# Half of the tokens' cross attention and expert queries placed among the first tile's expert picks, and norms on turned sums

## The reference

```python
def first_block(x, mem, ...):
    x = x + conv_mixers(rms_norm(x, norm_mix_g), ...)
    mem_n = rms_norm(mem, norm_mem_g)                  # 256 memory rows
    x = x + memory_cross_attention(rms_norm(x, norm_xa_g), mem_n, w_q, w_kv, w_xo)   # 4 heads of 256
    x = x + peer_ffn(rms_norm(x, norm_peer_g), w_pq, subkeys, u, v)
    return rms_norm(x, final_norm_g)

def peer_ffn(h, w_pq, subkeys, u, v):
    q = einsum('bsd,dq->bsq', h, w_pq).reshape(b, s, 8, 2, 128)
    sub_scores = einsum('bshpc,pnc->bshpn', q, subkeys)
    top_s, top_i = top_k(sub_scores, 16)               # then the best 16 of the 16 x 16 sums
    fin_s, fin_pos = top_k(cand_s, 16)                 # 8 heads x 16 = 128 experts a token
    gates = softmax(fin_s)
    act = gelu(einsum('chkd,cd->chk', u[experts], h)) * gates
    return einsum('chk,chkd->cd', act, v[experts])
```

## Time and profile before

| what | value |
| --- | --- |
| median of 3 runs | 3723.98 us (3719.53 to 3728.15) |
| the profiled execution | 3720.78 us |
| its span in the trace | 3719.0 us |
| PE busy | 3313.2 us, 89% |
| DVE busy | 2575.6 us, 69% |
| ACT busy | 1516.6 us, 41% |
| granted TensorE clock, mean | 0.962 |

### The profile page before, as it was taken

The page is one execution under the profiler, slowest core; times in us unless marked ns, Lnnn a source line. Parts: engine busy times, 40 slices in busy tenths (PEclk is TensorE's granted clock), DMA queues, the critical chain, the costliest instruction groups (busy, mean ns, idle before and its releaser), DMA issues.

```text
span 3719.0 us, 48652 instructions
## 1 busy us (share of the span) xinstructions
PE 3313.2 (89%) x17936; PEld 2559.5 (69%) x17936; DVE 2575.6 (69%) x4483; ACT 1516.6 (41%) x3014; POOL 872.7 (23%) x596
## 2 busy tenths in 40 slices
PE   7998989887777777699999999888996999999898
PEld 5886777672222222488777777667896988899898
DVE  6998252396776767677777777778855676768665
ACT  3222334323333333444444444544543444444443
POOL 1001443336656565222122232122100000000000
PEclk9999999999999999899999999899997999999999
DMA  3222222219999999699888899778955553453454
GB/s 119 95 95 74 97 97 85 70 63 414 417 381 419 383 420 390 266 381 386 344 316 322 299 373 386 276 288 337 368 182 178 189 164 126 128 185 118 131 186 154
DMA packets 178838, 901.92 MB, mean 243 GB/s; under 512 B 20944, under 2 KB 26320, under 8 KB 112672
## 3 DMA queue, kind: packets, MB, share of 16 engines
q0 software_dynamic: 73728, 536.90, 36.2%
q1 hardware_dynamic: 94640, 341.88, 26.8%
q10 hardware_dynamic: 10240, 20.12, 1.7%
HBM read 891.02 MB, written 7.80 MB: 242 GB/s over the span
## 4 chain that ended last, share of the span: by engine, by line
PE 65%; DVE 12%; DMA 7%; issue 6%; POOL 5%; ACT 3%; ACTq 0%; DVEq 0%; POOLq 0%
PE psum L650 50%; PE psum L894 9%; DMA buffer_float<-in_peer_uv,buffer_uint 6%; POOL buffer_float L2686 5%; DVE buffer_bfloat L2171 2%; DVE buffer_float L1849 1%; ACT slabs_rounded L1231 1%; PE psum L1100 1%; DVE buffer_float32r L1809 1%; DVE norm_mean_square L1840 1%; DMA raw_slabs<-in_slabs 1%; PE psum L1085 1%; DVE buffer_float L2120 1%; PE psum L1146 1%; DVE norm_recip_root L1817 1%
## 5 line engine op out<-in xcount | busy, mean ns | idle before, releaser
L650 PE MATMUL psum<-buffer_float32r,slabs_rounded 128*128 128x256 f32 (+2 forms) x9376 | 2025.8, 314 | 90.0 <-DVE buffer_float32r L1809 71.5
L650 PEld LDWEIGHTS psum<-buffer_float32r,slabs_rounded 128*128 128x128 f32 x9376 | 1532.2, 191 | 261.6 <-issue 144.8
L650 PE MATMUL psum<-buffer_float32r,slabs_remainder 128*128 128x256 f32 (+2 forms) x4688 | 1436.1, 306 | 0.0
L1887 DVE TENSOR_TENSOR slabs_remainder<-raw_slabs,slabs_rounded 128x1024 fp32r<-128x1024 f32 x570 | 696.1, 1224 | 494.2 <-ACT slabs_rounded L1231 485.6
L894 PE MATMUL psum<-buffer_float,buffer_float 128*128 128x512 f32 x1712 | 849.2, 623 | 190.2 <-ACT buffer_float L1438 159.6
L1231 ACT ACTIVATE slabs_rounded<-raw_slabs 128x1024 fp32r<-128x1024 f32 x650 | 684.2, 1056 | 732.5 <-PE psum L650 662.7
L2686 POOL DMA_INDIRECT buffer_float<-in_peer_uv,buffer_uint x512 | 676.7, 1322 | 1182.5 <-PE psum L894 684.0
L650 PEld LDWEIGHTS psum<-buffer_float32r,slabs_remainder 128*128 128x128 f32 x4688 | 894.0, 191 | 40.7
L2171 DVE CUSTOM_DVE_ANT_0 buffer_bfloat<-buffer_float,buffer_float 128x1024 bf16<-128x1024 f32 x512 | 625.8, 1222 | 226.7 <-DMA buffer_float<-in_peer_uv,buffer_uint 221.2
L894 PEld LDWEIGHTS psum<-buffer_float,buffer_float 128*128 128x128 f32 x1712 | 305.9, 196 | 618.7 <-issue 610.3
L2673 POOL TENSOR_TENSOR slabs_remainder<-raw_slabs,slabs_rounded 128x1024 fp32r<-128x1024 f32 x80 | 195.7, 2455 | 624.2 <-ACT slabs_rounded L1231 624.2
(11 more groups left out here) (202 smaller groups left out, 1914.6 us busy)
## 6 DMA issues: line engine op xcount, KB each, us to landing
raw_slabs<-in_slabs SPq DMA_DIRECT2D x650, 512.0 KB, 3.7
buffer_float<-in_peer_uv,buffer_uint POOLq DMA_INDIRECT x512, 9.7
buffer_float<-kept ACTq DMA_DIRECT2D x1, 5248.0 KB, 18.2
xT<-in_xT ACTq DMA_DIRECT2D x4, 512.0 KB, 5.4
buffer_float<-in_consts ACTq DMA_DIRECT2D x8, 256.0 KB, 3.3
kept<-buffer_float ACTq DMA_DIRECT2D x4, 512.0 KB, 5.2
kept<-buffer_float ACTq DMA_DIRECT2D x4, 272.0 KB, 4.2
kept<-buffer_float ACTq DMA_DIRECT2D x8, 136.0 KB, 3.1
```

The lines of the kernel that those rows point to most:

```text
L650: m = pe.matmul(out, a, b, start=start and j == 0, stop=stop and j == 2)
L1887: dve.tensor_tensor(slab_l[:, r, :], raw[:, r, :], slab_h[:, j, :].bitcast(F32), ALU.subtract)\
```

## The change

**The tokens are halved from cross attention on.** Steps 2 and 3 of the list above are done for the first 256 tokens alone. Keys and values, which are of the memory, are made once, and kept for all four heads. The other 256 tokens' queries, scores, softmax, sums, `w_xo` products, norm, expert queries and sub-scores are cut into 44 steps (`second_half`), which stand at 44 of the first 120 picks of tile 0 (`STEPS`). PE does a step behind `weigh(n)`; ACT and DVE do theirs one pick later, behind `coefficient(n + 1)` and `dot(n + 1)`. 32 of the steps hold a product of one slab with 256 columns: 8 queries, 8 outputs and 16 expert queries. Their slabs are loaded a second time (`AGAIN`, `SOURCE`), so the kernel loads 682 slabs for 650. In these steps DVE makes the slab remainders.

**The choices are paced otherwise.** Those of tile 1 (114 steps) go over the first 120 picks, those of tiles 2 and 3 (228 steps), whose sub-scores come from `second_half`, over the picks from 120 to 247.

**The norms work on turned sums.** PE puts the summed squares on the partitions as the stationary matrix against one column of ones (`mean_squares`), which gives one value a token in a few columns. Scale, root and reciprocal run on 128 x 4 values or fewer, and PE spreads the result over all partitions again (`spread`), in a PSUM bank that DVE reads in the norm's products. There are sixteen norms now, since that ahead of the experts is made twice.

```diff
+AGAIN = [*range(QUERIES, QUERIES + 8), *range(OUTS, FIRST)]
+BLOCK1 = FIRST + len(AGAIN)
+STEPS = [*range(1, 25, 3), *range(25, 35, 2), *range(35, 59, 3), *range(59, 69, 2), *range(69, 117, 3), 117, 119]
 def choices_by(n):
-    return min(3 * CHOICES, (n + 1) * 3 * CHOICES // CHOICE_PACE)
+    if n < PICKS - 8:
+        return (n + 1) * CHOICES // (PICKS - 8)
+    return min(3 * CHOICES, CHOICES + (n + 9 - PICKS) * 2 * CHOICES // (PICKS - 8))
...
+            def half_product(x, since=None, per=1):
+                bn = grab(gm)
+                w = Slab()
+                for k in range(KT):
+                    if since is not None and k % per == 0:
+                        pe.wait_ge(split, since + k // per + 1)
+                    m = w.add(psum[:, bn[0], 0:HALF], k, cols(x, k, 0, HALF), k == 0, k == KT - 1)
+                m.then_inc(bank_full[bn[0]], 1)
+                return bn
...
+                for j, (c, n) in enumerate(columns(T)):
+                    m = pe.matmul(psum[0:n, b, j:j + 1], norm_rs[:, c:c + n], ones[:, 0:1], start=True, stop=True)
...
+                for j, (c, n) in enumerate(columns(T)):
+                    m = pe.matmul(psum[:, b, c:c + n], turned_recip[0:n, j:j + 1].to_broadcast([n, P]),
+                                  ident[0:n, 0:n], start=True, stop=True)
...
             for n in range(PURE):
                 weigh(n)
+                if n in STEPS:
+                    next(steps)
...
+            def head_query(g, n, d):
+                b = full(gm.take())
+                act.activation(xq[g][:, n, d * HALF:(d + 1) * HALF], psum[:, b, 0:HALF], ACT.Copy)\
+                    .then_inc(bank_free[b], 1)
+                split_ahead()
...
+                for k in range(KT):
+                    b, n = gm.take()
+                    split_ahead()
+                    act.wait_ge(bank_free[b], n + 2)
+                    act.activation(squares_b[:, k, :], xT[:, k, META + HALF:T2], ACT.Square).then_inc(norm_sq, 1)
+                    yield
...
                     coefficient(n)
+                    if n - 1 in STEPS:
+                        next(steps)
...
+                def point(s):
+                    slab_remainder(FIRST + s + 3)
+                def query(s):
+                    gm.take()
+                    point(s)
...
+                for k in range(KT):
+                    bn = gm.take()
+                    point(8 + k)
+                    b = full(bn)
+                    x = xT[:, k, META + HALF:T2]
+                    dve.tensor_tensor(x, psum[:, b, 0:HALF], x, ALU.add).then_inc(bank_free[b], 1)
...
                 dot(n)
                 ...
+                if n - 1 in STEPS:
+                    next(steps)
...
             for j in range(B2):
-                dve.tensor_copy(sub_s[:, :, j, :], psum[:, b, :].rearrange("p (t n) -> p t n", t=QT))\
-                    .then_inc(bank_free[b], 1)
+                step(dve.tensor_copy(subs[0][:, j, :], psum[:, b, 0:P]))
+                step(dve.tensor_copy(subs[1][:, j, :], psum[:, b, P:2 * P]))
```

More of the change, by code:

```diff
@@ new lines, in subscores, with peer_query @@
+            def subscores(g, j):
+                emptied(sub_banks[j])
+                b = claim(at)
+                for t in range(2):
+                    m = pe.matmul(psum[:, b, t * P:(t + 1) * P], pq[g][:, j % 4, t * P:(t + 1) * P],
+                                  subk[:, j % 2, :], start=True, stop=True)
+                m.then_inc(bank_full[b], 1)
+            def peer_query(g, j, since):
+                sub_banks[j] = half_product(xop[g], None if j else since)
+                if j:
+                    subscores(g, j - 1)
@@ L918, in _ @@
                     turn_rows(first_sums, [at.take(), at.take()])
+            assert next(steps, None) is None and slabs.value() == BLOCK1
             turn_rows(list(sums_at), [at.take(), at.take()])
@@ L1206, in _, with turned_roots @@
             norms, splits = [0], [0]
+            def turned_roots(T):
+                act.wait_ge(norm_mean, norms[0] + 1)
+                for rows, a, b in turned_columns(T):
+                    act.activation(turned_root[0:rows, a:b], turned_ms[0:rows, a:b], ACT.Sqrt).then_inc(norm_root, 1)
+                norms[0] += 1
             def full(bn):
@@ L1397, in _, with peer_query @@
+            head_values()
+            head_sums(0, 2)
+            head_turned(0, 3)
+            head_sums(0, 3)
+            splits[0] += XA_HEADS
             split_ahead()
             act.dma_start(subk, subk_d).then_inc(subk_loaded, 16)
-            norm(xT, off=META, made=[[gm.take()] for _ in range(KT)], then=(1,) * 7 + (0,))
+            norm(xT, ((0, HALF),), off=META, dst=xop[0], made=[[gm.take()] for _ in range(KT)], then=(1,) * 7 + (0,))
+            def peer_query(g, j):
+                b = full(gm.take())
+                act.activation(pq[g][:, j % 4, :], psum[:, b, 0:HALF], ACT.Copy).then_inc(bank_free[b], 1)
@@ L1986, in _, with skip @@
             add_to_stream()
+            def skip(ring, n):
+                for _ in range(n):
+                    ring.take()
             def head_values(n):
@@ L2155, in _ @@
                         pass
-            for _ in range(2 * QT):
-                at.take()
+            skip(at, 4)
             drained(at)
@@ L2204, in _ @@
                     turned = [at.take(), at.take()]
-            assert next(choosing, None) is None
+            assert next(choosing, None) is None and next(steps, None) is None
             add_rows(1, turned)
```

797 lines of the change are left out of this document (490 added, 307 removed).

## The result

The changed kernel takes 3808.7 us, the median of four runs (3807.3 to 3813.3), against 3723.2 for the kernel before on the same chip: ratio 1.0228, 95% interval 1.0215 to 1.0240. Run again later (e12) it took 3814.5, ratio 1.0243 (1.0223 to 1.0264). It is slower by 85 to 90 us. Its profiled execution took 3808.0 us, span 3806.2.

What follows compares the result with a forecast made beforehand. PE was taken to bound cross attention, DVE the choices, and the gathers the picks of tiles 0 and 1. The sum -89 - 12 + 180 + 5 = +84 on 3720.8, plus 3.2, gave 3808 us, with 3783 to 3833 at chance 0.5.

Steps and rivals of the forecast that it cites:

- Front: Everything ahead of tile 0's picks, with products, scores and norms on half the tokens: 89 us less.
- The choices' stage: Expert queries with tile 0's choices, ahead of the gathers: 3 us less, 17 us either way.
- Norms: Ten norms of the second block, about 1.2 us less each: 12 us less, at least 0, at most 17.
- Tile 0: Picks with the second half's steps among them: 509 us for 329, 180 more; bounds 40 and 203.
- the chain: In tile 0's query steps, a later pick's dot waits for product, copy, rounding and remainder; cycle 11.3 us before clock falls.
- The output cycle: Tile 0's output steps: PE waits 1.3 us and a cycle takes 9.5; 8 steps, 76 us.
- Tile 1: More choice steps a pick on DVE make the gathers stop longer: 5 us more, at least 0, at most 20.
- Rival 1: The gathers stay the bound in tile 0, which grows by 40 us: 3668 us; chance 0.14.
- Rival 2: In tile 0 the chain holds but PE's clock doesn't fall, 41 us less: 3767 us; chance 0.19.
- Rival 3: POOL's remainders hit DVE's choices twice a head (+17), each clock fall costs 2.65 (+23): 3848 us; chance 0.1.
- Rival 4: Half a gain: shorter chain in tile 0, cycle about 10, near the old time, 3700 to 3745 us; chance 0.07.
- The signs I had named: First gather near 747, choices each 12 to 13 us; in tile 0 DMA share near 0.7, PE's clock under 0.85.

Runs made afterwards that it cites:

- e12: The changed kernel itself run again, with nothing changed: 3814.5 us, ratio 1.0243.
- e8: Changed kernel with rounding ahead of the copy, sub-scores' copy a step later, and VectorE making 16 slab remainders instead of GpSimd: 3708.1 us, ratio 0.9964.
- e4: Kernel before with turned sums in all norms, block 1's and block 2's, and nothing else of the change: 3711.3 us, ratio 0.9963.
- e11: Kernel before with turned sums in block 2's norms alone: 3716.0 us, ratio 0.9979.
- e5: Kernel before with turned sums in block 1's norms alone: 3714.2 us, ratio 0.9977.
- e1: Changed kernel with ScalarE rounding the next slab ahead of the product's copy in tile 0's head-query and expert-query steps: 3727.3 us, ratio 1.0005.
- e2: As e1, and VectorE copies each expert-query step's sub-scores one step later: 3717.1 us, ratio 0.9974.
- e3: Changed kernel with six extra matmuls in PE's wait of each of tile 0's 16 expert-query cycles: 3796.0 us, ratio 1.0192.
- e7: As e2, and in the 8 output steps VectorE adds and ScalarE squares each product one step later: 3713.3 us, ratio 0.9977.
- e6: Changed kernel with each of the 32 slabs that are read again loaded twice in a row: 3816.3 us, ratio 1.0256.
- e9: Changed kernel with the edits of e2, e7 and e8 together: 3700.5 us, ratio 0.9941.
- e10: Kernel before with turned sums in all norms and VectorE making the last 16 slabs' remainders ahead of the gathers: 3710.4 us, ratio 0.9964.

## Why the forecast held

It held in its mechanism, and in its sum by luck as well: the front gained 9 us less than forecast and tile 0 cost 10 less, which cancel, so that 3808 and 3808.7 agree far better than the terms do.

- **Front, -89; measured -80.4.** Up to the last output's add (628.50 for 699.19) it is -70.7, of which I had 67 with the first norm. From there to the first choice it is 19.1 us for 34.5, where I had 15.5. The choices' stage was mis-sized: -3 forecast, +6.0 measured, well within my 17 either way. The rival's two hits a head came about in part: the first head has three stretched instructions, the next four have two each (one of these only to 1.26 us), the last three none. The choices began 17.4, 13.9, 14.4, 14.9 and 14.5 us apart while POOL's remainders ran, 10.7 us behind the last of them. The kernel before had one in each of seven heads, so 11 hits stand against 7. e8 prices the 11 at 22 us for the stage, e4's trace the 7 at 14.5; the difference of 7 is most of the 9 by which the term was off.
- **Norms.** Of 13.8 us (e4), block 2 has 7.8 (e11) where I had 12, block 1 has 8.6 (e5) where I had 2 for the first norm, 3 for the cross-attention one, and the expert norm's within the 19. The conformer's gained nothing, as said (ACT's roundings in e4 are 3.2 us ahead before it and 3.1 behind it).
- **Tile 0, +180; measured +170.4.** By the stretches: head queries 108.0 (112 forecast), attention 35.0 (41), outputs 84.5 (76), norm 23.8 (30), expert queries 217.8 (214), the rest 33.1 (36). The steps of attention and of the norm were too dear by 6 us each and the outputs too cheap by 8.5, luck again in part; and the length before is 331.8 between the same instructions, where I had 329. The cycle of an expert query was 13.50 us (13.35), the wait 3.14 (3.0), the fall of the clock 1.70 (1.7). e1 and e2 show that the chain is the cause: without the rounding in it 81 us go, without the sub-scores' copy 10 to 12 more, with all of the reading, weighing and products unchanged. e3 shows the clock's share.
- **The output cycle, 9.5**, was 9.62 on PE where it ran free (942.65 to 952.28), but 10.6 on average: e7 took 0.7 of it away; the rest I have not tried to explain.
- **Tile 1, +5; measured +5.2.** What follows: -8.1 in these two traces, but the same program differs by 8 between two executions, so this number is no evidence; e11's is.
- **Rival 1** (the gathers stay the bound) was to decide below a mean cycle of 9.7 us. It is refuted for the changed kernel by e6. In e2's and e9's expert queries it is right, with a cycle of 9.3 us, and both kernels are faster than the kernel before; but tile 0 grows by 75 and 68 us there, not by the 40 of this rival. **Rival 2** (no fall of the clock) is refuted by e3; its price of 41 was 24 times 1.7; the trace has 21 falls, 15 in the expert queries at 1.7 each and six in the head queries for 9.3 us together, some 35 us in all. **Rival 3** was in part right, with more hits (at about 7 us and not 17) and without the dearer falls. **Rival 4** is where e1 landed (3727.3 us, cycle 9.72).
- **The signs I had named.** First gather near 747: 755.8. PE's clock under 0.85 in tile 0: it was 0.93 and 0.89. A fall that costs 1.7 us in a cycle of 13.5 leaves even the stretch of the expert queries at 0.88, and the rest of the tile higher; the step from the price of a fall to that sign was wrong, not the price. DMA share near 0.7: 0.82 and 0.76. Choices begun each 12 to 13 us: no, see **Front**. ACT's rounding 0.3 us behind the product's end: 1094.42 for 1094.12.

## What to carry to other kernels

When work is woven into a stream of small dependent steps, write down for each engine what stands in its queue between one small step and the next, and take out whatever waits for a long product: moving a rounding ahead of a copy in two places here was worth as much as the 80 us that the whole split gained in front. Ask of each rounding, copy and add whether it can go one step earlier or later than the product it is written beside; here all three could. And where VectorE sets the pace, look for what GpSimd costs it: here 1.6 us for each 2.4 us instruction with the split, more than the 1.22 that VectorE needs to do the work itself, and 1.04 without it, less than that.

## What the runs showed of the hardware

- The same wait of PE, 3.14 us, was followed by a lower clock (0.73 in the mean of the next 1.5 us, 5.37 us for two picks) in most cycles and by the full clock in others (3.67 us; at 1167.05 in the first profile and at 1112.21 in e12's, and behind 3.28 us at 846.20). Behind the waits of 1.08 to 1.43 us ahead of two picks the tiles 0 of the changed kernel and of e1 show no fall; behind 1.97 us e12 has one (1259.40), behind 2.00 us the kernel before has none (1249.13), behind 2.29 us e1 has one (826.53), and behind 2.31 none (804.52). Which of the longer ones are hit, the traces don't tell.
- The fall came inside the pair: granted clock 1.00 in 1085.90 to 1086.40, 0.50 in 1087.40 to 1088.00.
- A VectorE instruction of 0.42 us took 2.45 us when it began 0.2 us behind a GpSimd subtraction of 2.36 us, and ended 0.3 us behind it. In the choices' stage 11 VectorE instructions were stretched beside 14 such subtractions in the changed kernel, 7 beside 14 in the kernel before, and none in e8 and e10, which have no subtraction there.
- Two executions of one program differed by 8 us in the last 2200 us, 2204.7 and 2212.8, while the 500 us of tile 0 agreed within 1 us.
